# The first modulation multiplied in 32-bit form from the raw chunks, four column quarters of TensorE at a time

## The reference, cut to what matters

```
mod_in, modc_in = silu(c), silu(c_ctx)                    # two vectors of 2048
sh1, sc1, ... = split(mod_in  @ w_mod + b_mod, 6)         # w_mod: 2048 x 12288
csh1, csc1, ... = split(modc_in @ w_mod + b_mod, 6)
h  = rmsnorm(x,   g_attn) * (1 + sc1)  + sh1
hc = rmsnorm(ctx, g_attn) * (1 + csc1) + csh1
cq, ckv, kr, qn, kn, vn, f = split_columns(h @ w_in)      # and the same for hc
...                                                       # attention, FFN, a second block
```

## Time and profile before

| | us |
|---|---|
| median of 3 runs (2754.77 to 2756.59) | 2756.56 |
| the profiled execution: its own time | 2755.58 |
| its span | 2753.7 |
| PE busy | 2637.1 (96%) |
| DVE busy | 1828.7 (66%) |
| ACT busy | 1280.7 (47%) |
| POOL busy | 32.5 (1%) |

### The profile page before, as it was taken

One profiled execution on the slowest core, in us unless ns is written; L12 is line 12 of the kernel. 1 busy time (PEld: TensorE's weight loads), 2 busy tenths in 40 slices (PEclk: granted clock), 3 DMA queues, 4 the chain that ended last, 5 costly groups with the idle time before them and its releaser, 6 DMA issues.

```text
span 2753.7 us, 38067 instructions
## 1 busy us (share of the span) xinstructions
PE 2637.1 (96%) x15638; PEld 2292.3 (83%) x15638; DVE 1828.7 (66%) x2479; ACT 1280.7 (47%) x1671; POOL 32.5 (1%) x26
## 2 busy tenths in 40 slices
PE   6999998989999999999799999989899999999997
PEld 4778866878888888888688899977788888888886
DVE  7776875778888877555755555567666566565555
ACT  6752243445555555444444455544444444444432
POOL 1110000000000000000000000000000000000000
PEclk9999999999999999999899999999999999999998
DMA  8877874657777755555355544445555555555553
GB/s 295 308 264 274 300 266 137 226 180 233 244 231 239 226 191 187 191 188 193 132 186 182 185 152 143 134 137 171 175 168 189 189 190 190 191 190 190 188 190 107
DMA packets 152365, 547.27 MB, mean 199 GB/s; under 512 B 16896, under 2 KB 20864, under 8 KB 151424
## 3 DMA queue, kind: packets, MB, share of 16 engines
q1 hardware_dynamic: 149712, 540.35, 59.2%
q10 hardware_dynamic: 2480, 4.49, 0.5%
HBM read 542.68 MB, written 2.10 MB: 198 GB/s over the span
## 4 chain that ended last, share of the span: by engine, by line
PE 92%; DVE 5%; ACT 2%; issue 1%; DMA 0%; SPq 0%; DVEq 0%; ACTq 0%
PE ps L430 41%; PE ps L429 21%; PE ps L434 3%; PE ps L435 3%; PE ps L436 3%; PE ps L427 2%; PE ps L1873 2%; PE ps L1875 2%; PE ps L1877 2%; DVE lo L384 2%; PE ps L442 2%; PE ps L440 2%; PE ps L441 2%; PE ps L428 1%; PE ps L1659 1%
## 5 line engine op out<-in xcount | busy, mean ns | idle before, releaser
L384 DVE TENSOR_TENSOR lo<-raw,hi 128x1024 fp32r<-128x1024 f32 x886 | 1089.8, 1236 | 810.5 <-ACT hi L371 808.0
L371 ACT ACTIVATE hi<-raw 128x1024 fp32r<-128x1024 f32 x886 | 932.1, 1059 | 1219.7 <-PE ps L430 902.9
L430 PE MATMUL ps<-pair,hi 128*128 128x512 f32 x3614 | 1261.6, 393 | 0.0
L429 PE MATMUL ps<-pair,lo 128*128 128x256 f32 x3614 | 1013.1, 280 | 6.1 <-DVE pair L1399 4.2
L430 PEld LDWEIGHTS ps<-pair,hi 128*128 128x128 f32 x3614 | 681.1, 188 | 147.6
L429 PEld LDWEIGHTS ps<-pair,lo 128*128 128x128 f32 x3614 | 681.5, 189 | 9.7 <-issue 4.6
L430 PE MATMUL ps<-hid,hi 128*128 128x512 f32 x1376 | 477.4, 392 | 0.0
L429 PE MATMUL ps<-hid,lo 128*128 128x256 f32 x1376 | 384.6, 280 | 0.0
L430 PEld LDWEIGHTS ps<-hid,hi 128*128 128x128 f32 x1376 | 258.3, 188 | 56.8
L429 PEld LDWEIGHTS ps<-hid,lo 128*128 128x128 f32 x1376 | 258.3, 188 | 0.3
L1140 DVE TENSOR_REDUCE tmp<-ps 128x256 f32<-128x512 f32 x272 | 183.2, 684 | 9.5 <-PE ps L430 9.1
(11 more groups left out here) (282 smaller groups left out, 2511.4 us busy)
## 6 DMA issues: line engine op xcount, KB each, us to landing
raw<-in_stream SPq DMA_DIRECT2D x1014, 512.0 KB, 3.6
xc<-in_xc SPq DMA_DIRECT2D x4, 1024.0 KB, 8.1
x<-in_x ACTq DMA_DIRECT2D x1, 2048.0 KB, 9.0
outT<-x SPq DMA_DIRECT2D x4, 512.0 KB, 3.0
c_bc<-in_c_bc SPq DMA_DIRECT2D x1, 1024.0 KB, 7.3
bias<-in_rpb ACTq DMA_DIRECT2D x4, 256.0 KB, 4.5
raw<-in_stream SPq DMA_DIRECT2D x2, 256.0 KB, 3.8
dft<-in_dft_tab ACTq DMA_DIRECT2D x1, 512.0 KB, 5.8
```

What stands on the lines that cost most here:

```text
L371: e.activation(hi[:, c % R, :], raw_of(p), ACT.Copy).then_inc(hi_ready, 1)
L384: e.tensor_tensor(lo[:, c % R, :], raw_of(p), hi[:, c % R, :].bitcast(F32), ALU.subtract)\
L429: e.matmul(out[:, T:2 * T], wlo, act[:, 0, :], start=False, stop=False)
L430: return e.matmul(out, whi, both_, start=False, stop=last)
```

## The change

The mod chunks are no longer split. TensorE takes the raw chunk as float32 moving operand. The stationary operand `csil` has 32 columns (two of data, 30 of zeros that POOL writes at the start), and the four k-tiles of a chunk go to four column quarters of the array, into four quarters of bank 6's partitions. `turn_mod` sums the quarters, since `pick` now has four unit blocks and the contraction runs over 128 rows. The raw buffer of a mod chunk is given back when its matmuls are done (`mod_used`). At the start the squares are shared out between DVE and POOL, and the square-root table is loaded ahead. The order of the work on every engine of the stage is written anew. The stream's order of chunks stays.

```
+QUAD = 32
+POOL_SQ = (2, 5, 8, 11)
@@ SP, load(p): what a raw buffer waits for
+                    if kind == "mod":
+                        e.wait_ge(mod_used, i + 1)
+                    elif kind == "weights":
                         e.wait_ge(lo_ready, i + 1)
@@ POOL
+            e.memset(csil[:], 0.0).then_inc(csil_zeroed, 1)
+            for j, kt in enumerate(POOL_SQ):
+                e.wait_ge(sqx_piece, kt + 1)
...
+                    e.tensor_tensor(sq_acc[:, 1], sq_acc[:, 1], src, ALU.add).then_inc(sqx_pool, 1)
@@ ACT
+            e.activation(csil[:, :, 0:2], cvec[:].rearrange("p v t -> p t v"), ACT.Silu).then_inc(silu_c, 1)
+            e.preload_act_table_set("sqrt_and_others")
...
             for kt in range(KT):
-                to = mod_end(kt) + 4
-                split_hi(e, at, to)
-                at = to
                 rows(kt)
                 if kt:
                     first_hi(kt - 1)
+                if kt >= LAG:
+                    split_hi(e, kt - LAG, kt - LAG + 1)
@@ DVE
             for kt in range(1, KT):
-                split_lo(e, at, mod_end(kt) + 2)
                 modulation(kt - 1)
-                at = mod_end(kt) + 5
-                split_lo(e, mod_end(kt) + 2, at)
+                if kt >= LAG:
+                    split_lo(e, kt - LAG, kt - LAG + 1)
                 first_lo(kt - 1)
             modulation(KT - 1)
+            split_lo(e, KT - LAG, KT - LAG + 1)
@@ PE
+            def modulate(kt):
+                for i in range(4):
+                    p = POS[("mod", 4 * kt + i)]
+                    e.wait_ge(landed[p % RR], 16 * (p // RR + 1))
                     if i == 0 and kt:
                         e.wait_ge(mod_rows, kt)
+                    w = raw_of(p).rearrange("p (k n) -> p k n", k=4)
                     for k in range(4):
+                        m = e.matmul(ps[QUAD * k:QUAD * (k + 1), 6, 0:2 * P], csil[:, 4 * i + k, :], w[:, k],
+                                     start=(i == 0), stop=(i == 3))
+                    m.then_inc(mod_used, 1)
...
+            modulate(0)
+            e.wait_ge(sqx_added, len(DVE_SQ) + 1)
             e.matmul(ps[:, 5, :], ones, sq_acc[:, 0].rearrange("p v t -> p (v t)"), start=True, stop=True).then_inc(sqx_sum, 1)
             for kt in range(1, KT):
-                mod_half(kt, 0)
+                modulate(kt)
                 turn_mod(kt - 1)
-                mod_half(kt, 1)
                 if kt >= LAG:
                     first(kt - LAG)
```

More of the change, by code:

```diff
@@ L26 @@
 CPG = KT // 2
+QUAD = 32
+POOL_SQ = (2, 5, 8, 11)
+DVE_SQ = [kt for kt in range(KT) if kt not in POOL_SQ]
 EPS = 1e-6
@@ L64, in _stage @@
     CHUNKS.extend((name, i) for i in range(n))
[L67 to L72, removed]
+_stage("a", KT - 1)
+CHUNKS += [("kr", 0), ("a", KT - 1), ("kr", 1)]
 for _s, _n in (("kn", CPG), ("vn", CPG), ("uqn", 4), ("uqr", 2), ("ukn", 4), ("ukv", 4), ("f", CPG), ("qn", CPG),
@@ L80 @@
 BASE = {s: AT[(s, 0)] for s in dict.fromkeys(q[0] for q in CHUNKS)}
-def mod_end(kt):
-    return AT[("mod", 4 * kt + 3)]
 N_EXTRA = 2 * 4 * KT
@@ L104 @@
 SEQ = []
-for _c in range(N_CHUNKS):
+for _kt in range(KT):
+    SEQ.extend(("mod", 4 * _kt + _i) for _i in range(4))
+    if LAG <= _kt:
+        SEQ.append(("weights", _kt - LAG))
+for _c in range(KT - LAG, N_CHUNKS):
     SEQ.append(("weights", _c))
@@ L164, in host_tables @@
     pick = np.zeros((P, 2), f)
-    pick[0:4] = np.tile(np.eye(2, dtype=f), (2, 1))
+    for j in range(4):
+        pick[QUAD * j:QUAD * j + 2] = np.eye(2, dtype=f)
     base = np.concatenate([np.eye(P, dtype=f), np.ones((P, P), f), pick], axis=1)
@@ L215, in two_blocks @@
         base, _ = place("base", [P, 2 * P + 2])
[L216 removed]
+        ident, ones, pick = base[:, 0:P], base[:, P:2 * P], base[:, 2 * P:2 * P + 2]
         vecs, _ = place("vecs", [P, NV])
         cvec, _ = place("cvec", [P, 2, KT])
[L219 to L220 removed]
+        csil, _ = place("csil", [P, KT, QUAD])
         mrows, _ = place("mrows", [P, 2, 2 * P])
@@ L309, in two_blocks @@
         hi_ready, lo_ready, weights_used, extra_used = sem("hi_ready"), sem("lo_ready"), sem("weights_used"), sem("extra_used")
-        silu_c, c_ready, csplit_hi, csplit_lo = sem("silu_c"), sem("c_ready"), sem("csplit_hi"), sem("csplit_lo")
+        silu_c, c_ready, csil_zeroed, mod_used = sem("silu_c"), sem("c_ready"), sem("csil_zeroed"), sem("mod_used")
+        sqx_pool = sem("sqx_pool")
         sqx_piece, sqx_added, sqx_sum, stdx, rinvx = sem("sqx_piece"), sem("sqx_added"), sem("sqx_sum"), sem("stdx"), sem("rinvx")
@@ L588, in _ @@
         def _(e):
+            e.memset(csil[:], 0.0).then_inc(csil_zeroed, 1)
+            e.wait_ge(csil_zeroed, 1)
             e.memset(kre[64:P, :, :], 0.0).then_inc(zeroed, 1)
@@ L591, in _ @@
             e.wait_ge(zeroed, 2)
+            for j, kt in enumerate(POOL_SQ):
+                e.wait_ge(sqx_piece, kt + 1)
+                src = tmp[:, 2 * (j % 2):2 * (j % 2) + 2, :]
+                if j == 0:
+                    e.tensor_copy(sq_acc[:, 1], src).then_inc(sqx_pool, 1)
+                else:
+                    e.wait_ge(sqx_pool, j)
+                    e.tensor_tensor(sq_acc[:, 1], sq_acc[:, 1], src, ALU.add).then_inc(sqx_pool, 1)
             e.wait_ge(rinvx, 1)
@@ L610, in _ @@
             e.wait_ge(s_c, 16)
-            e.activation(csil[:], cvec[:].rearrange("p v t -> p t v"), ACT.Silu).then_inc(silu_c, 1)
-            e.wait_ge(silu_c, 1)
-            e.activation(csplit[:, :, 0:2], csil[:], ACT.Copy).then_inc(csplit_hi, 1)
+            e.wait_ge(csil_zeroed, 1)
+            e.activation(csil[:, :, 0:2], cvec[:].rearrange("p v t -> p t v"), ACT.Silu).then_inc(silu_c, 1)
+            e.preload_act_table_set("sqrt_and_others")
             def rows(kt):
-                e.wait_ge(weights_used, mod_end(kt) + 1)
+                e.wait_ge(mod_used, 4 * kt + 4)
                 if kt >= 2:
                     e.wait_ge(mod_turned, kt - 1)
-                e.activation(mrows[0:4, kt % 2, :], ps[0:4, 6, 0:2 * P], ACT.Copy).then_inc(mod_rows, 1)
+                e.activation(mrows[:, kt % 2, :], ps[:, 6, 0:2 * P], ACT.Copy).then_inc(mod_rows, 1)
             def first_hi(kt):
@@ L632, in _ @@
                 e.wait_ge(s_xc[kt // 4], 16)
[L633 to L636, removed]
+                if kt in POOL_SQ:
+                    j = POOL_SQ.index(kt)
+                    if j >= 2:
+                        e.wait_ge(sqx_pool, j - 1)
+                    dst = tmp[:, 2 * (j % 2):2 * (j % 2) + 2, :]
+                else:
+                    i = DVE_SQ.index(kt)
+                    if i >= 2:
+                        e.wait_ge(sqx_added, i - 1)
+                    dst = sq_slot[:, i % 2]
+                e.activation(dst, xc[:, kt], ACT.Square).then_inc(sqx_piece, 1)
             e.wait_ge(s_vecs, 16)
@@ L651, in _ @@
                     e.activation(c_bc[:], c_bc[:], ACT.Silu).then_inc(c_ready, 1)
-            split_hi(e, at, at + 1)
+            split_hi(e, KT - LAG, KT - LAG + 1)
             first_hi(KT - 1)
-            at += 1
+            at = KT - LAG + 1
             to = BASE["kn"] + 2
@@ L989, in first_lo @@
                                 ALU.subtract).then_inc(xc_lo, 1)
-            for kt in range(KT):
+            for i, kt in enumerate(DVE_SQ):
                 e.wait_ge(sqx_piece, kt + 1)
-                if kt == 0:
+                if i == 0:
                     e.tensor_copy(sq_acc[:, 0], sq_slot[:, 0]).then_inc(sqx_added, 1)
                 else:
-                    e.wait_ge(sqx_added, kt)
-                    e.tensor_tensor(sq_acc[:, 0], sq_acc[:, 0], sq_slot[:, kt % 2], ALU.add).then_inc(sqx_added, 1)
-            split_lo(e, 0, 2)
+                    e.wait_ge(sqx_added, i)
+                    e.tensor_tensor(sq_acc[:, 0], sq_acc[:, 0], sq_slot[:, i % 2], ALU.add).then_inc(sqx_added, 1)
+            e.wait_ge(sqx_added, len(DVE_SQ))
+            e.wait_ge(sqx_pool, len(POOL_SQ))
+            e.tensor_tensor(sq_acc[:, 0], sq_acc[:, 0], sq_acc[:, 1], ALU.add).then_inc(sqx_added, 1)
             e.wait_ge(stdx, 1)
             e.reciprocal(rinv[:], rinv[:]).then_inc(rinvx, 1)
-            split_lo(e, 2, 4)
             e.wait_ge(s_vecs, 16)
-            at = 4
             for kt in range(1, KT):
-                split_lo(e, at, mod_end(kt) + 2)
                 modulation(kt - 1)
-                at = mod_end(kt) + 5
-                split_lo(e, mod_end(kt) + 2, at)
+                if kt >= LAG:
+                    split_lo(e, kt - LAG, kt - LAG + 1)
                 first_lo(kt - 1)
             modulation(KT - 1)
+            split_lo(e, KT - LAG, KT - LAG + 1)
             first_lo(KT - 1)
+            at = KT - LAG + 1
             to = BASE["kn"] + 2
@@ L1439, in _ @@
             e.wait_ge(s_base, 16)
[L1440 to L1445, removed]
+            e.wait_ge(silu_c, 1)
+            def modulate(kt):
+                for i in range(4):
```

(11 more changed lines are left out.)

8 lines of the change are left out of this document (removed).

## The result

The changed kernel takes 2807.3 us (median of 4 runs, 2806.6 to 2808.4) against 2756.6 us: the ratio is 1.0186, 95% interval 1.0168 to 1.0204. It is slower by 51 us; 2805 were forecast. The profiled execution took 2808.4 us with a span of 2806.6, which is 52.9 us more than before.

A forecast was written before the change was run, and what follows sets the result against it. PE (TensorE) was taken to bound the stage. Rounds 13 x (13.45 - 9.09) = +56.7, start -9.7, tail +2 gave +49 us on 2755.6, say 2805 us (65%); range 2774 to 2832.

The forecast's parts named there:

- What bounds it: 13 rounds of the stage: PE bound, busy 113.4 of 118.1 us; the 64 splits removed from DVE and ACT gain nothing.
- The chain: Between turn and `first`, PE waits for modulation, first_hi, hi and lo over three engines: 4.5 us in every round.
- The modulation: 16 float32 matmuls a round in four column quarters: 2.0 us, replacing 3.9 us of float32r matmuls.
- The bound of 1.7: Modulation of a round if four quarters gain fully: 6.8 / 4 = 1.7 us; in series 6.8 us.
- the 0.3 us set aside for passages: In each round's modulation: three passages from one form of matmul to another, 0.1 us each.
- The clock: PE's clock falls to half rate in nearly every round's pause, costing about 2.0 us each: a round of 13.45 us.
- Start and tail: `first(0)` begins at 36 us, a gain of 9.7 us; `first(13)` to `first(14)` takes 7.4 against 5.38, costing 2 us.
- Modulations 1 and 2 fit beside it: At the start, they run beside the path to `first(0)`, 2.0 to 3.4 us each.
- The clock that stays up: Rival, 13%: no clock fall in the rounds, a round of 11.45 us, +22 us, 2778 us.
- the weaker quarters: Rivals for the modulation: twofold gain, 3.4 us, 2827 us, 12%; in series, 6.8 us, 2871 us, 4%.
- The faster one: Rival, 6%: "a" split ready ahead of the turn's chain, no pause, a round of 6.9 us, 2718 us.
- The limit given for breaking even: Pause ahead of `first` must be under 2.3 us to break even at the full clock, 9.7 us a round.

The follow-up runs named there:

- the kernel with the hi part ahead: Against the changed kernel, only ACT's hi part of chunk (a, kt-2) moved ahead of rows(kt) and first_hi(kt-1), DVE's lo part left: 2755.0 us, ratio 0.9998.

## Why the prediction was right

**What bounds it.** That DVE's and ACT's lighter load could give back next to nothing held, but it was put at exactly nothing, and that was read too quickly: in the 13 rounds of before PE waited 5.1 us for `lo`, 0.4 us a round. Ten of the 13 rounds took 8.6 to 8.8 us, and the mean of 9.09 comes from three with waits. In the changed kernel this is swallowed by the pause.

**The chain.** 4.5 us of pause was the sum of rows; 4.50 is what stands ahead of each of `first(0)` to `first(13)`, with the links in the predicted order and of the predicted lengths (0.39, 0.09, 2.70 and 1.31 us). That the order makes it, and not the 32-bit form, was argued then and is shown now: with the order undone and the form kept, the time falls by 70 us.

**The modulation.** 2.0 us were taken, 1.87 measured. The bound of 1.7 was nearer than the 2.2 us estimated with the Trainium skill ("TensorE: Matmul & The Clock Gate", Part 3), and the run with one quarter puts the gain from four at 7.03 / 1.87 = 3.8 times, above the 3.07 that the Trainium skill has there for four row tiles. For the drain at a change of tiling mode, which the Trainium skill states ("TensorEngine Tiling (Array Packing)", Key Properties), a round leaves little room: 1.87 - 1.71 = 0.16 us behind the matmuls of the modulation, where 1.71 is 8 x 0.213, and 0.09 us ahead of them (98.28 to 98.60, less the 0.23 from one matmul of `first` to the next). The 0.3 us set aside for passages was thus on the high side; the 0.39 us of L434's first record, from which it was taken, is no price of each passage, since that of `first(13)` in the earlier trace rows lasts 0.28.

**The clock.** 2.0 us a round were forecast from two pauses of the earlier trace rows; 2.3 us is what filling the pause gave back. The window from 474 in the earlier trace rows was misread: 0.64 on average puts the fall at 474.3 and not 474.6, 2.5 us into the pause, which changes no term of the sum. That the clock's fall was its own cost, beside the pause, is shown by two pairs of runs with the same chain.

**Start and tail.** -9.7 us were forecast for `first(0)`, -9.0 came (36.74 us). The path was another one than forecast: DVE was done with `first_lo(0)` at 30.3 us, a microsecond earlier than my sum has it, but `modulation(1)` then had to wait for `turn_mod(1)`, which stands behind the last chunk of `modulate(2)`. That one began at 30.21 us, behind a landing:

```profile
30.21 1.08 PE L1464 MATMUL ps<-raw,csil 128*32 128x256 f32 x8 [0.20 <-DMA raw<-in_stream]
32.27 0.16 DVE L993 TENSOR_TENSOR first_mod<-ps,vecs 128x4 f32<-128x4 f32 x1 [1.99 <-PE ps L1473]
```

"Modulations 1 and 2 fit beside it" was thus the step that failed here, and that it and the early `first_lo(0)` come to 0.7 us together is luck.

The tail was put at 2 us and is 3.3: from `first(13)` to `first(14)` 8.67 us, since the clock's share is larger here than I took.

**The sum.** The rounds are 178.1 - 118.1 = +60.0, start -9.0, tail +3.3: +54.3, less 1.4 us that come back later, is the 52.9 of the span. The terms forecast were 56.7, -9.7, and 2; the errors of the rounds (+3.3), the start (+0.7) and the tail (+1.3) all have one sign and are 5.3 us together; those of the rounds and the tail come from the clock, which took 0.3 to 0.4 us a round more than forecast, against 0.13 less for the modulation. The 1.4 us that come back later make it 3.9, and the median of after lies 1.1 us below its profiled execution: that it came within 2.3 us of the forecast is partly luck.

**The rivals.** The clock that stays up and the weaker quarters are out. The faster one, a pause that does not come, was wrong in this kernel because of the order of the splits. Its price of 2718 us, for a round of 6.9, was too low for that order alone: with the splits ahead as before, the round was 8.64 us and the time 2737, since the chunk landed too late for it: the price counted the rate of the loads (6.4 us for five chunks), not when they are asked for. The best order, with the stream changed too, reached 2723 with 7.5. The limit given for breaking even is a slip as well: 9.7 us a round leaves 9.7 - 6.9 = 2.8 us of pause at the full clock, not 2.3. With the clock's falls added, the kernel with the hi part ahead broke even at a pause of 1.58. Where I erred on the way was in the experiments: I took a pause of 1.6 us for harmless, and the run with the hi part ahead came out 16 us over its first number.

## What to carry to other kernels

Taking work off engines that aren't the bound gains next to nothing, and in moving what is left one can put it behind a longer chain: for each instruction moved, look at what now stands ahead of it on its own engine and what that waits for. Here an operand of the next matmul was put behind a chain through TensorE itself. Undoing that order alone took 70 us off and made the change 18 us faster than the kernel before; with the stream's order changed and the splits a round earlier it was 29. A pause of TensorE can also cost more than its length, 4.5 + 2.3 us a round here. If it cannot be closed, filling it with matmuls of no use can pay, as long as they end before the operand comes.

## What the runs showed of the hardware that was not expected

- A pause of 1.58 us in a round of 8.5 to 10 us, behind a turn of 0.60 us, was followed by a fall of TensorE's clock to 1.2 GHz in 11 of 13 rounds: 0.85 on average over 104 us. With the pause filled the clock is at 1.00, with the same turn. In the kernel before, waits of up to 1.2 us in the 13 rounds left it at 1.00.
- The 16 float32 matmuls of a round, in four column quarters with different moving data, take 1.87 us, and 7.03 us all in one quarter.
- DVE's additions and subtractions are longer when they start while POOL does an operation of two tensors: those of 128x512 float32 took 1.34 to 1.57 us and not 0.69, and the split of 128x1024 took 2.19 and not 1.22. Moving a quarter of the additions to POOL ended no sooner (20.2 against 19.8 us).
- Ahead of the first change of the clock that the trace holds (21.9 us in the changed kernel) PEclk shows 1.00, but eight records of the modulation take 1.08 us there (from 17.86 us), as at 30.21 us at half rate, and 0.64 us at 26.37 us. So PEclk says nothing of the start.
